# Both query units of the sparse attention as seven block products behind the key units, with the dilated tables and the tail laid out anew

## What is computed

```python
h = rmsnorm(x, norm_mix); proj = h @ w_in
q_a, kv_a, g_a, qkv_b, g_m = split(proj)
y_a = nsa_attention(q_a, kv_a, sigmoid(g_a), ...)   # 8 heads: compressed, selected and window branch
for (window, dil) in ((128, 1), (512, 4), (2048, 16)):   # 12 heads, 4 for each group
    s = q_g @ k_g.T - slope * delta * dil      # banded, causal, on the tokens of one residue
    o_g, lse_g = softmax(s) @ v_g
y_b = sum(o_g * softmax(lse over the groups))
x = x + (sigmoid(g_m[0]) * (y_a @ w_up_nsa) + sigmoid(g_m[1]) * (y_b @ w_up_dil)) @ w_out
x = x + (silu(gate) * up) @ w_ffn_out          # gate, up = rmsnorm(x, norm_ffn) @ w_ffn_in
return rmsnorm(x, norm_final)
```

## Time and profile before

| | |
|---|---|
| median of three runs | 768.67 us |
| profiled execution | 767.3 us, span 765.5 us |
| granted clock of TensorE | 0.998 |
| PE busy | 754.8 us, 99% |
| DVE busy | 579.6 us, 76% |
| ACT busy | 368.2 us, 48% |
| POOL busy | 173.1 us, 23% |

### The profile page before, as it was taken

The page is one execution under the profiler, slowest core; times in us unless marked ns, Lnnn a source line. Parts: engine busy times, 40 slices in busy tenths (PEclk is TensorE's granted clock), DMA queues, the critical chain, the costliest instruction groups (busy, mean ns, idle before and its releaser), DMA issues.

```text
span 765.5 us, 14070 instructions
## 1 busy us (share of the span) xinstructions
PE 754.8 (99%) x5606; PEld 683.7 (89%) x5606; DVE 579.6 (76%) x1065; ACT 368.2 (48%) x690; POOL 173.1 (23%) x130
## 2 busy tenths in 40 slices
PE   9999999999999999999999999999999999999996
PEld 7879999889887787788888989999999999999995
DVE  5998972654875777666733689999999998799865
ACT  6233255254456566753322974444444444555434
POOL 1305220000000000001210037777766653000000
PEclk9999999999999999999999999999999999999999
DMA  7921436250311110116342533444433422224532
GB/s 231 347 94 57 138 83 165 58 170 4 111 56 57 57 56 6 38 46 189 125 150 56 181 95 89 122 121 112 111 111 111 111 83 81 101 95 165 177 100 110
DMA packets 104640, 83.63 MB, mean 109 GB/s; under 512 B 16976, under 2 KB 94848, under 8 KB 104576
## 3 DMA queue, kind: packets, MB, share of 16 engines
q1 hardware_dynamic: 104336, 82.46, 35.8%
q10 hardware_dynamic: 240, 0.29, 0.1%
HBM read 77.44 MB, written 5.29 MB: 108 GB/s over the span
## 4 chain that ended last, share of the span: by engine, by line
PE 95%; DVE 2%; issue 1%; POOL 1%; DMA 0%; ACT 0%; ACTq 0%; DVEq 0%; POOLq 0%
PE bank L2163 25%; PE bank L2165 25%; PE bank L2164 24%; PE bank L2448 3%; PE bank L2467 2%; PE bank L2696 2%; PE bank L2695 2%; PE bank L2694 2%; PE bank L2435 2%; PE bank L2349 1%; POOL weight_sums L749 1%; PE bank L2390 1%; PE bank L2371 1%; PE bank L2312 1%; PE bank L2204 1%
## 5 line engine op out<-in xcount | busy, mean ns | idle before, releaser
L1294 DVE TENSOR_TENSOR w_lo<-w_raw,w_hi 128x2048 fp32r<-128x2048 f32 (+2 forms) x26 | 57.6, 2217 | 73.2 <-ACT w_hi L797 73.0
L749 POOL TENSOR_TENSOR weight_sums<-w_raw 128x512 f32<-128x512 f32 x42 | 71.4, 1700 | 142.7 <-PE bank L2165 92.6
L2163 PE MATMUL bank<-n_hi,w_hi 128*128 128x512 f32 x224 | 89.9, 402 | 0.0
L2165 PE MATMUL bank<-n_hi,w_lo 128*128 128x512 f32 x224 | 87.4, 390 | 0.0
L2164 PE MATMUL bank<-n_lo,w_hi 128*128 128x512 f32 x224 | 87.4, 390 | 0.0
L770 POOL TENSOR_TENSOR n_lo<-merge_tmp,n_hi 128x512 fp32r<-128x512 f32 x8 | 10.4, 1296 | 268.8 <-ACT n_hi L1030 268.8
L797 ACT CAST w_hi<-w_raw 128x2048 fp32r<-128x2048 f32 (+2 forms) x26 | 47.9, 1841 | 33.9 <-PE bank L2165 23.2
L1875 DVE TENSOR_TENSOR sums_lo<-weight_sums,sums_hi 128x1024 fp32r<-128x1024 f32 x38 | 63.3, 1708 | 0.3 <-ACT sums_hi L1090 0.3
L2163 PE MATMUL bank<-w_hi,n_hi 128*128 128x256 f32 (+2 forms) x192 | 62.2, 324 | 0.9 <-issue 0.9
L2163 PE MATMUL bank<-t_hi,sums_hi 128*128 128x256 f32 x228 | 62.9, 276 | 0.0
L2164 PE MATMUL bank<-t_lo,sums_hi 128*128 128x256 f32 x228 | 62.9, 276 | 0.0
(11 more groups left out here) (360 smaller groups left out, 2370.4 us busy)
## 6 DMA issues: line engine op xcount, KB each, us to landing
w_raw<-in_w_ffn_in_dram SPq DMA_DIRECT2D x44, 512.0 KB, 5.0
w_raw<-in_w_in_dram SPq DMA_DIRECT2D x37, 512.0 KB, 4.7
w_raw<-in_w_ffn_out_dram SPq DMA_DIRECT2D x22, 512.0 KB, 3.5
w_raw<-in_w_out_dram SPq DMA_DIRECT2D x8, 512.0 KB, 4.0
w_raw<-in_w_in_dram SPq DMA_DIRECT2D x12, 256.0 KB, 4.5
xs<-in_x_dram SPq DMA_DIRECT2D x4, 512.0 KB, 5.2
wck_k<-in_w_ck_dram SPq DMA_DIRECT2D x1, 2048.0 KB, 11.8
wck_v<-in_w_cv_dram SPq DMA_DIRECT2D x1, 2048.0 KB, 13.6
```

The lines of the kernel that those rows point to most:

```text
L749: pool.tensor_tensor(s7[s][:, b], a0, a1, op).then_inc(s_sums, 1)
L1294: dve.tensor_tensor(wlo[u % 2][:, split_part(u)], raw[u % 2][:, 0:n], whi[u % 2][:, split_part(u)].bitcast(F32), ALU.subtract).then_inc(lo ...
L2163: pe.matmul(dst, w[0], x_[0], start=start, stop=False)
L2165: return pe.matmul(dst, w[1], x_[0], start=False, stop=stop)
```

## The change

QA moves to the units 7 and 8, ahead of VB (9 to 11), and KEY_UNITS becomes 4 to 8: both QA units are computed as seven block products right after the dilated keys. The four QA tiles vanish from the list of fillers, so BESIDE_DIL_SCORES is (3, 3, 2, 2) and BESIDE_CMP starts with 2. POOL's sums of the units 6, 7 and 8 wait until the low halves of the unit before are done. The dilated tables are made in two steps: DVE prepares three masks in `keys(4)` (`dil_masks`), and ACT makes the twelve tables from them in `keys(8)` after `split_hi(9)` (a copy with a scale). The tail runs the steps 20 and 21 together for each token tile, and DVE computes the second half of each row's result in one operation in place of `gained`.

```diff
-KEY_UNITS = (4, 5, 6)
+KEY_UNITS = (4, 5, 6, 7, 8)
...
-U_CMP, U_QB, U_KB, U_VB, U_QA, U_KA, U_VA, U_GM, U_UP, U_WO, U_IN = 0, 1, 4, 7, 10, 12, 13, 14, 22, 26, 30
+U_CMP, U_QB, U_KB, U_QA, U_VB, U_KA, U_VA, U_GM, U_UP, U_WO, U_IN = 0, 1, 4, 7, 9, 12, 13, 14, 22, 26, 30
...
-BESIDE_DIL_SCORES = (3, 3, 3, 4)
+BESIDE_DIL_SCORES = (3, 3, 2, 2)
...
-BESIDE_CMP = (3, 1, 0, 0, 2, 0, 0, 0, 1)
+BESIDE_CMP = (2, 1, 0, 0, 2, 0, 0, 0, 1)
...
-    jobs += [("keys", U_KB), ("cmp_kv", 0), ("keys", U_KB + 1), ("keys", U_KB + 2)]
+    jobs += [("keys", U_KB), ("cmp_kv", 0)] + [("keys", u) for u in KEY_UNITS[1:]]
...
             for u in KEY_UNITS[1:]:
+                if u > KEY_UNITS[1]:
+                    pool.wait_ge(lo_done, u)
                 if u - 2 in KEY_UNITS:
...
+            def dil_bias():
+
+                act.wait_ge(dbias_made, 3)
+                for h in range(4):
+                    for g, (a, b) in enumerate(((0, 256), (256, 384), (384, 512))):
+                        ins = act.activation(dbias[:, h, a:b], dbias[:, 3, a:b], ACT.Copy,
+                                             scale=-SLOPE_DIL[g][h] * min(DIL[g], 4))
+                ins.then_inc(dbias_made, 1)
...
-            def dil_bias():
+            def dil_masks():
...
-                for h in range(4):
-                    for g, (a, b, mask) in enumerate(((0, 256, mask0[:]), (256, 384, cmask[:, 384:512]), (384, 512, mask2[:]))):
-                        ins = dve.scalar_tensor_tensor(
-                            out=dbias[:, h, a:b], in0=dist[:, 512 - (b - a):512],
-                            scalar=-SLOPE_DIL[g][h] * min(DIL[g], 4), in1=mask, op0=ALU.mult, op1=ALU.add)
-                link(ins)
+                for a, b, mask in ((0, 256, mask0[:]), (256, 384, cmask[:, 384:512]), (384, 512, mask2[:])):
+                    dve.scalar_tensor_tensor(out=dbias[:, 3, a:b], in0=mask, scalar=-1024.0, in1=dist[:, 512 - (b - a):512],
+                                             op0=ALU.mult, op1=ALU.add).then_inc(dbias_made, 1)
...
                 dve.tensor_tensor(key_u2[:], ps[a + 1][:, 256:512], key_m1u4u3[:, 0, :], ALU.add).then_inc(u2_made, 1)
+                if k == 0:
+                    dil_masks()
...
                 if not more:
                     keys_out(u, 1)
-                    dil_bias()
...
                 g, tiles = DIL_STEPS[n % 4]
+                if n == 0:
+                    dve.wait_ge(dbias_made, 4)
...
-                tile_evacuated(LAST_TILE[U_KB + 1 if n == 0 else U_KB + g])
+                tile_evacuated(LAST_TILE[U_QA if n == 0 else U_QA + 1])
...
             square(0)
             root(0)
+            final_scale(0)
             square(2)
             root(2)
-            final_scale(0)
+            final_scale(2)
             square(1)
             root(1)
-            final_scale(2)
             square(3, 0)
-            final_scale(1)
             square(3, 1)
             root(3)
-            act.wait_ge(r3_ready, TT)
-            act.activation(xg[:, 3, 0:512], xg[:, 3, 0:512], ACT.Copy, scale=st[:, 3, 3:4]).then_inc(fin_ready, 1)
+            final_scale(1)
+            final_scale(3)
...
-            def gained(t, first, cols=slice(0, 512)):
...
+            def final_half(t):
...
+                dve.scalar_tensor_tensor(out=xg[:, t, 512:1024], in0=x3[1][:, t, :], scalar=st[:, 3, t:t + 1],
+                                         in1=gfin[:, 512:1024], op0=ALU.mult, op1=ALU.mult).then_inc(last_ready, 1)
...
-            for n in (OUT_N - 2, OUT_N - 1):
-                out_ready(n)
-                for t in TAIL_TILES[:2]:
+            for t in TAIL_TILES[:3]:
+                for n in (OUT_N - 2, OUT_N - 1):
+                    out_ready(n)
```

More of the change, by code:

```diff
@@ L79 @@
 VA_N = 280
-U_CMP, U_QB, U_KB, U_VB, U_QA, U_KA, U_VA, U_GM, U_UP, U_WO, U_IN = 0, 1, 4, 7, 10, 12, 13, 14, 22, 26, 30
+U_CMP, U_QB, U_KB, U_QA, U_VB, U_KA, U_VA, U_GM, U_UP, U_WO, U_IN = 0, 1, 4, 7, 9, 12, 13, 14, 22, 26, 30
 SLOT = KC * VA_N
-TILES = [(u, a) for u in range(U_UP) for a in range(4 if u in (7, 8, 9, 13) else 2)]
+TILES = [(u, a) for u in range(U_UP) for a in range(4 if u in (9, 10, 11, 13) else 2)]
 FIRST_TILE = {u: TILES.index((u, 0)) for u in range(U_UP)}
@@ L503, in slot_used @@
         def slot_used(n):
+            if n == OUT_N - 1:
+                return m_done, 7 * N7 + n - 5
             return (m_done, 7 * N7 + n - 1) if n >= 2 else (m_done, 7 * sevens(FT - 2 + n) + 7)
         def w_block(ring, n):
-            return ring[n % 2][:, 0:1024].rearrange("p (b c) -> p b c", b=4)
+            first = 1024 if n == OUT_N - 1 and ring is not raw else 0
+            return ring[n % 2][:, first:first + 1024].rearrange("p (b c) -> p b c", b=4)
         def out_cols(j):
@@ L566, in load @@
                     else:
-                        c = C_KC if u == U_CMP else C_QB + 256 * (u - U_QB) if u < U_QA else C_GM + 256 * (u - U_GM)
+                        c = C_GM + 256 * (u - U_GM)
+                        if u < U_KA:
+                            c = C_KC if u == U_CMP else C_QB + 256 * (u - U_QB - (2 if u >= U_VB else 0))
                         for k in (0, 4):
@@ L1453, in tile @@
                         dst = gm[:, 2 * (u - U_GM) + a, :]
-                    scale = QSCALE if u < U_KB or U_QA <= u < U_KA else 1.0
+                    scale = QSCALE if u < U_KB else 1.0
                     dve.scalar_tensor_tensor(out=dst, in0=src, scalar=scale, in1=row,
@@ L1556, in keys_out @@
                 dve.wait_ge(done, k + 1)
-                dst, src, row = of_group(kb, k, part, bank, rrow[:])
-                dve.scalar_tensor_tensor(out=dst, in0=src, scalar=1.0, in1=row,
+                if u < U_QA:
+                    dst, src, row = of_group(kb, k, part, bank, rrow[:])
+                else:
+                    dst, src, row = qa[:, 2 * (u - U_QA) + part, :], bank, rrow[:]
+                dve.scalar_tensor_tensor(out=dst, in0=src, scalar=1.0 if u < U_QA else QSCALE, in1=row,
                                          op0=ALU.mult, op1=ALU.mult).then_inc(tile_evac_dve, 1)
@@ L2086, in _ @@
                 elif n == 19:
+                    w_parts_lo(21)
                     first_gained(2)
@@ L2114, in last_mean, with mean_of @@
                                          in1=st[:, 0, 7:8], op0=ALU.mult, op1=ALU.add).then_inc(part_ready, 1)
+            def mean_of(t):
+                k = TAIL_TILES.index(t)
+                total = ss_end[:, 0:1] if t == 3 else st[:, 2, 4 + t:5 + t]
+                dve.wait_ge(x3_ss, TT + (5 if t == 3 else k + 1))
+                dve.wait_ge(part_ready, 2 if t == 3 else 1)
+                link(dve.scalar_tensor_tensor(out=st[:, 0, t:t + 1], in0=total, scalar=1.0 / D,
+                                              in1=st[:, 0, 4 + t:5 + t], op0=ALU.mult, op1=ALU.add))
             def inverse_root(t):
@@ L2129, in inverse_root @@
                 dve.tensor_tensor(st[:, 3, t:t + 1], w, y, ALU.mult).then_inc(r3_ready, 1)
[L2131 to L2136 removed]
+            def final_half(t):
+                k = TAIL_TILES.index(t)
+                dve.wait_ge(r3_ready, k + 1)
+                dve.wait_ge(x3_sum, X3_BASED + (5 if t == 3 else k + 1))
+                dve.scalar_tensor_tensor(out=xg[:, t, 512:1024], in0=x3[1][:, t, :], scalar=st[:, 3, t:t + 1],
+                                         in1=gfin[:, 512:1024], op0=ALU.mult, op1=ALU.mult).then_inc(last_ready, 1)
             early_part()
             residual_part(0)
[L2139 to L2140 removed]
+            mean_of(0)
+            inverse_root(0)
             residual_part(2)
[L2142 to L2143 removed]
+            final_half(0)
+            mean_of(2)
             inverse_root(2)
             residual_part(1)
[L2146 removed]
+            final_half(2)
             residual_part(3, 0)
[L2148 removed]
+            mean_of(1)
             inverse_root(1)
```

69 lines of the change are left out of this document (26 added, 43 removed).

## The result

The change takes 770.31 us (median of 20 runs) beside 768.27 for the kernel before (20 runs): a ratio of 1.0023, with an interval of 1.0016 to 1.0031. The profiled execution took 770.68 us with a span of 768.9.

A forecast was written before the change was run, and what follows sets the result against it. PE bounds the kernel, busy for 754.8 of 765.5 us. Terms -21.8 + 18.6 + 2.4 - 0.9 + 2.3 - 1.1 = -0.5, added to the median of 768.67, gave 768.2; range 764.6 to 772.4.

The forecast's parts named there:

- The step that failed: Six mask operations on DVE in keys(4): some 1.7 us in idle time, costed at nothing unless POOL delays them.
- The rival that I gave 0.22: Masks alternate with POOL's sums in unit 5, taking 5.5 in place of 1.7: +3.0, 771.7 us; chance 0.22.
- The key units: Two key units added on PE at 9.6 each, less 0.6 for unit 5's wait: +18.6 us.
- the loop: POOL's sums and DVE's low halves wait for each other in units 6 to 8, 10.1 to 11.1 a turn: +2.4 us.
- The wait of unit 5: PE's wait in key unit 5 for DVE's second `sums_lo` should go: -0.6 us, counted within the key units.
- The first merge: With less filler, PE waits 0.5 to 2.8 us before the first turn; busy queue taken: +2.3.
- The second half: The second merge keeps its fillers less one QA tile; cover and chain within 1 us, costed at nothing.
- The VB wait: PE's wait of 0.94 at 107.42 in the dilated stage, for a low half of VB weights, goes: -0.9 us.
- the tail: At the kernel's end, ACT's row scale and DVE's gain products leave the chain: -1.1 us, bounds 0 and -1.3.

The follow-up runs named there:

- masks_after_kv: The change with the six mask operations moved from keys(4) to the end of cmp_kv on DVE; 768.24 us, ratio 0.9984 to the kernel before.
- warm_wait: The change with unit 5's second block product computed two more times ahead of PE's wait; 771.12 us, ratio 1.0035 to the kernel before.
- masks_late: The change with the six mask operations moved from keys(4) to keys(8); 766.17 us beside 769.41 for the kernel before, and 766.01 beside 768.24 when run again.
- no_pool_wait: The change without POOL's new wait for the low halves of the unit before; 773.47 us, ratio 1.0037 to the kernel before.

## Why the prediction was wrong

The forecast was 768.2, 0.5 us below the kernel before and called no change; measured were 2.0 us above it, inside the range but the other way.

**The step that failed** is that of the masks: "So their own length costs nothing, unless POOL, which is in its sums of unit 5 right then (70.23), delays them". POOL does delay them. The rival that I gave 0.22 is what happened, step by step: the masks took 5.5 us, u4u3 came at 74.5, where the rival said 75, the score step at 116.6, where it said 117. Four operations were held, where it counted three. Moving the masks away takes 4.1 us from the key units in the trace. I had argued against it from the 5.03 at 65.13, where POOL waited for DVE. The row was right and the reading too general: the operations that kept POOL out there were DVE's long low parts, and the short masks did not keep it out.

**The key units and the loop** were sized well: with the masks out of the way they take 40.3, where the terms gave 20.26 + 18.6 + 2.4 = 41.3. I gave the loop 0.5 to 1.5 over a unit in each turn, and units 7 and 8 are 0.9 and 1.1 over; unit 6 had no wait. One turn takes 10.6, inside my 10.1 to 11.1. That the loop carries a delay on to every later unit held too: POOL's first sum of unit 6 starts 8.95 us after unit 5 in the change and 5.48 with the masks late, 3.5 apart. In the change itself PE loses 4.3 in unit 5 already (13.94 beside 9.68), by its wait and the clock, so its lag at the score step needs no loop. What shows the loop are `masks_after_kv`, where a start 1.4 later gives a score step 1.4 later, and `warm_wait`, 3.5 and 3.6.

**The wait of unit 5** I had put down to `sums_lo` alone. It went, but in the change PE waits in the same unit for `cmp_kv`'s evacuations, which stand behind the masks on DVE; I had not listed PE among those that wait for them, nor the 1.5 us of half clock behind that wait.

**The first merge** was mis-sized: +2.3 taken, with a busy queue; the trace has 0 at the turn and 0.5 ahead of it. The read of vb left the queue before the merge's write, so the quiet 1.9 was the price, and my own lower bound, a chain of 12.2 and a wait of 0.5, was right: the chain took 12.3. The fixed cost of a DMA that the Trainium skill gives (DMA: Bandwidth & Descriptors, "Anatomy of one DMA"), some 2.0, is near the 1.9 too. That section is written for transfers that GpSimd issues, and these go out on SP's queue.

**The second half** was costed at nothing and lost 1.5. I had looked at the merge's cover and not at DVE's order ahead of it: with one tile fewer in the list, the low half of the GM unit falls in front of the last score step. These two misses nearly cancel, which is luck.

**The VB wait and the tail** came as forecast: no wait is left at the second VB unit's first tile, and the tail gave 1.3 for 1.1.

With the feed-forward's 1.1 and the masks' 4.1 left out, the 3.4 of the stages become 1.8 below the kernel before, and `masks_late` measured 2.2 and 3.2 below in its two runs. The saving of the change was there; one place of six short operations took it all back and 2 us more.

Open: why the masks let POOL in and the low parts did not. That three of the masks wait for the one before was my first guess, but in `no_pool_wait` the fifth, which waits for none, was held for 1.37 as well. Why the feed-forward's start order falls one way or the other was not tried, and neither was another place for the masks between the late one and the two that cost.

## What to carry to other kernels

Before you put short operations into a gap of one engine, look at what its neighbour on the shared port pair does in that gap: six operations of 0.2 to 0.4 us took 5.5 beside GpSimd's sums. Where two engines wait for each other round a loop that takes as long as the unit of work or longer (here 10.6 us beside 9.6), a delay ahead of it is not absorbed but carried to its end, so the place for such work is behind the loop. And when fillers leave a list, read what each engine now does ahead of the steps that stay, not the length of the cover alone.
